# Four modulation rows of a second layer computed in the grid attention instead of the latent attention

## The reference, cut to what matters

```python
for i in range(DEPTH):
    m_lat = jnp.split((c_lat @ w_mod[i] + b_mod[i])[:, None, :], N_MOD, axis=-1)   # N_MOD = 6, w_mod: 2 x 1024 x 6144
    m_ctx = jnp.split(c_con @ w_mod[i] + b_mod[i], N_MOD, axis=-1)
    h_lat = modulate(x_lat, g_pre_mix[i], m_lat[0], m_lat[1])
    ...
    x_lat = x_lat + m_lat[2] * rms_norm(y_lat, g_post_mix[i])
    f_lat = channel_mlp(modulate(x_lat, g_pre_mlp[i], m_lat[3], m_lat[4]), w_mlp_in[i], w_mlp_out[i])
```

## Time and profile before

| what | value |
|---|---|
| three runs, median (lowest to highest) | 2287.1 us (2286.93 to 2288.31) |
| profiled execution: its own time, its span | 2291.53 us, 2290.2 us |
| busy PE | 2230.3 us, 97% of the span |
| busy DVE, ACT, POOL | 1240.3 us (54%), 1019.6 us (45%), 565.2 us (25%) |
| chain that ended last, by engine | PE 77%, DVE 10%, POOL 6%, ACT 5% |
| mean granted TensorE clock | 0.994 of full speed |
| moved by DMA | 344.54 MB, 149 GB/s over the span |

### The profile page before, as it was taken

The page is one execution under the profiler, slowest core; times in us unless marked ns, Lnnn a source line. Parts: engine busy times, 40 slices in busy tenths (PEclk is TensorE's granted clock), DMA queues, the critical chain, the costliest instruction groups (busy, mean ns, idle before and its releaser), DMA issues.

```text
span 2290.2 us, 34957 instructions
## 1 busy us (share of the span) xinstructions
PE 2230.3 (97%) x15237; PEld 1958.2 (86%) x15237; DVE 1240.3 (54%) x1486; ACT 1019.6 (45%) x1226; POOL 565.2 (25%) x465
## 2 busy tenths in 40 slices
PE   9999899999999999999999999999999999999999
PEld 8889898978889889778889966898888898678999
DVE  5766566657655665477556456352223264565443
ACT  5544345445543454455444366343322334554442
POOL 3323444331330231231232210011211200231221
PEclk9999999999999999999999999999999999999999
DMA  8555445456555555786555310132232242114552
GB/s 282 184 175 184 158 147 165 155 199 200 188 187 188 177 197 167 255 300 219 181 189 178 102 38 19 40 127 92 92 106 96 92 142 74 56 60 162 184 184 74
DMA packets 205234, 344.54 MB, mean 150 GB/s; under 512 B 8845, under 2 KB 69498, under 8 KB 205082
## 3 DMA queue, kind: packets, MB, share of 16 engines
q1 hardware_dynamic: 205082, 342.31, 45.6%
HBM read 341.24 MB, written 1.05 MB: 149 GB/s over the span
## 4 chain that ended last, share of the span: by engine, by line
PE 77%; DVE 10%; POOL 6%; ACT 5%; issue 2%; SPq 0%; DMA 0%; DVEq 0%; POOLq 0%; ACTq 0%
PE PS L472 74%; DVE WL L458 4%; PE PS L494 3%; ACT WH L442 2%; POOL small L1682 1%; POOL small L1680 1%; POOL TMP L1691 1%; POOL TMP L1076 1%; DVE TMP L1594 1%; DVE small L1572 0%; POOL TMP L1692 0%; DVE TMP L1047 0%; DVE TMP L1044 0%; DVE XB L704 0%; DVE TMP L1039 0%
## 5 line engine op out<-in xcount | busy, mean ns | idle before, releaser
L458 DVE TENSOR_TENSOR WL<-raw,WH 128x2048 fp32r<-128x2048 f32 (+2 forms) x281 | 653.7, 2347 | 651.6 <-ACT WH L442 651.6
L472 PE MATMUL PS<-XB,WH 128*128 128x256 f32 (+1 forms) x3392 | 898.6, 342 | 3.8 <-DVE XB L1138 1.1
L472 PE MATMUL PS<-XB,WL 128*128 128x256 f32 (+1 forms) x2368 | 687.9, 290 | 0.0
L472 PEld LDWEIGHTS PS<-XB,WH 128*128 128x128 f32 x3392 | 585.5, 189 | 84.1 <-issue 4.1
L442 ACT ACTIVATE WH<-raw 128x2048 fp32r<-128x2048 f32 (+2 forms) x281 | 515.5, 1858 | 263.7 <-PE PS L472 258.2
L472 PEld LDWEIGHTS PS<-XB,WL 128*128 128x128 f32 x2368 | 448.3, 189 | 8.7
L472 PE MATMUL PS<-WH,XB 128*128 128x256 f32 (+2 forms) x1888 | 379.2, 296 | 13.6 <-DVE WL L458 10.2
L472 PE MATMUL PS<-HB,WH 128*128 128x256 f32 (+1 forms) x1568 | 344.1, 309 | 1.0 <-DVE WL L458 1.0
L472 PEld LDWEIGHTS PS<-WH,XB 128*128 128x128 f32 x1888 | 306.3, 193 | 35.7 <-issue 16.0
L472 PE MATMUL PS<-WL,XB 128*128 128x256 f32 (+2 forms) x944 | 275.7, 292 | 0.0
L472 PEld LDWEIGHTS PS<-HB,WH 128*128 128x128 f32 x1568 | 255.7, 191 | 18.9 <-DVE WL L458 3.0
(11 more groups left out here) (256 smaller groups left out, 2189.3 us busy)
## 6 DMA issues: line engine op xcount, KB each, us to landing
raw<-in_ffn_w_in SPq DMA_DIRECT2D x88, 1024.0 KB, 5.2
raw<-in_w_mod SPq DMA_DIRECT2D x48, 1024.0 KB, 5.3
raw<-in_ffn_w_out SPq DMA_DIRECT2D x40, 1024.0 KB, 5.2
raw<-in_a_w_in SPq DMA_DIRECT2D x36, 1024.0 KB, 5.1
raw<-in_w_mlp_in SPq DMA_DIRECT2D x32, 1024.0 KB, 5.2
raw<-in_w_mlp_out SPq DMA_DIRECT2D x32, 1024.0 KB, 5.1
raw<-in_gla_w_in SPq DMA_DIRECT2D x12, 1024.0 KB, 5.2
raw<-in_attn_w_qkv SPq DMA_DIRECT2D x6, 1024.0 KB, 5.1
```

Source lines behind the costliest of these rows:

```text
L458: dve.e.tensor_tensor(self.WL[j % NRAW][:, 0:nk * nn], self.raw[j % NRAW][:, 0:nk * nn], wh.bitcast(F32), ALU.subtract).then_inc(*self.lo. ...
L472: return self.pe.e.matmul(out, l, r, start=start, stop=stop, skip_group_check=skip)
```

## The change

Latent attention: in steps -1, 0, 1 and 2 one modulation row less is placed on PE, ACT and DVE. Step -1 keeps two, steps 0 to 2 keep the first of two, step 3 keeps both. Grid attention: one row each is placed in the steps 25, 27, 29 and 31, on PE at the end of the step, on ACT behind the step's exponentials, on DVE in the step after, behind its scores. All four use bank 0 for the matmuls and bank 1 for the transposes. ACT copies the last one in step 33. The order of the rows stays, so the rows that move are the sixth to ninth of the second layer by number, which the gated linear attention and the second MLP use. The chunks of the moved rows stand in the stream between the last projection of the grid attention and its output projection now.

```diff
--- before.py
+++ after.py
@@ -1819,15 +1819,14 @@
             if own:
                 turn_p(hs, 2)
                 turn_p(hs, 3)
-            fill()
+            if hs not in (0, 1, 2):
+                fill()
             if own:
                 pv(hs, 2)
                 pv(hs, 3)
             if more:
                 turn(hs + 1, 1)
-            if hs < 0:
-                fill()
-            else:
+            if own:
                 self.empties([7], (self.o_done, ("lat", hs)))
         self.attn_out_pe("lat", self.aO, (self.o_done, ("lat", 3)), w_out)
 
@@ -1942,15 +1941,13 @@
                 self.fill_act(0)
                 self.act_settle()
                 turn(hs + 1, 0)
-            self.act_held = int(not more)
-            self.fill_act(0)
-            self.act_held = 0
-            self.act_settle()
+            if hs not in (0, 1, 2):
+                self.act_held = int(not more)
+                self.fill_act(0)
+                self.act_held = 0
+                self.act_settle()
             if more:
                 turn(hs + 1, 1)
-            if hs < 0:
-                self.fill_act(0)
-                self.act_settle()
         self.attn_out_act("lat", "f3", 40)
 
     def latent_dve(self):
@@ -2084,11 +2081,11 @@
                 turn_p(hs, 3)
             if more:
                 rotated(1, hs + 1)
-            self.dve_held = int(not more)
-            fill()
-            self.dve_held = 0
+            if hs not in (0, 1, 2):
+                self.dve_held = int(not more)
+                fill()
+                self.dve_held = 0
             if hs < 0:
-                fill()
                 continue
             dve.wait_ge(self.expd, ("lat", hs, 3))
             dve.e.reciprocal(rd, den).then_inc(*self.v_step.up(("lat", "recip", hs)))
@@ -2600,6 +2597,7 @@
 
 
 
+    GRID_FILLS = (25, 27, 29, 31)
     GRID_SPARE = {6: 2, 2: 3, 3: 6}
 
     GRID_STEPS = [(seg, 2 * pair + j, o) for seg in range(2) for pair in range(2) for o in range(2) for j in range(2)]
@@ -2756,6 +2754,8 @@
                 g, p = divmod(n - 2, 8)
                 for j in range(2):
                     turn_p(g, 2 * p + j)
+            if n in self.GRID_FILLS:
+                self.pe_mods.send((0, 1))
         self.rest_grid = self.last_products_pe("grid", w_o, self.x_both(("go0", "go1")), None, True)
 
     def grid_act(self):
@@ -2862,8 +2862,12 @@
             if n < 32:
                 score(g, 2 * p)
                 score(g, 2 * p + 1)
+            if n in self.GRID_FILLS:
+                self.fill_act(0)
             if p == 0:
                 next(nxt, None)
+            if n == 33:
+                self.act_settle()
             if 27 <= n < 33:
                 seg, g3 = divmod(n - 27, 3)
                 split(g3, seg)
@@ -2936,6 +2940,8 @@
             g, p = divmod(n, 8)
             if n < 32:
                 score(g, 2 * p)
+            if n - 1 in self.GRID_FILLS:
+                self.dve_mods.send(1)
             if n > 5 and n % 4 == 2:
                 out(*divmod(n // 4 - 1, 2))
             if n and n % 4 == 0:
```

## The result

The changed kernel takes 2319.28 us (2312.26 to 2323.21), the kernel before 2287.05 on the same chip: 1.0132 [1.0117, 1.0146], or 32 us by the medians. The profiled execution of after took 2312.26 us (span 2310.9), 20.7 more than the profiled execution of before.

A forecast was written before the change was run, and what follows sets the result against it. PE was taken to bound the kernel, so a move pays only where PE waits. Latent -1.5 plus grid +18.7 gave +17.2 us on the median of 2287.1: 2304.3 us, range 2296 to 2312.

The forecast's parts named there:

- The order on the lists: Latent and grid attention: places of splits and copies in the engines' lists cost -1.5 + 18.7 = +17.2 us together.
- Head 0: Latent attention, step -1: ACT splits in time, PE begins head 0 at about 970.3, gain 3.0 us.
- the scaling: Latent step 0: DVE's scaling, behind two splits, begins at 990.4 against 986.82; PE idles 3.4 us; step 1.7 us later.
- -1.5: Latent attention sum in us: -3.0 + 1.7 + 1.7 - 1.9, within a bound of -10.3 and +2.
- the first two terms: Grid attention: row at 25 costs +2.3 us, row at 27, waiting for ACT's copy, +4.6.
- 18.7: Grid attention sum in us: rows 2.3 + 4.6 + 5.4 + 4.4, and late output projection splits 2.0.
- The loads: Grid attention: loads of the moved rows' and the projection's chunks cost nothing, by the count of buffers.
- rival (3): Both attentions: clock falls behind PE's new waits; one or two falls of 5.1 us, 2309 to 2314 us; chance 0.20.
- (1): Grid attention: ACT's copies reach PE in time, rows cost only their work, +12.2 us, some 2297.8; chance 0.17.
- (2): Both attentions: cover holds, grid idle takes 4.43 us, latent gives back 10.3; -4.4, 2282.7 us; chance 0.10.

The follow-up runs named there:

- fillers: Changed kernel plus dummy matmuls on PE in the waits the change made, in both latent and grid attention: 2306.36 us, 1.0076 to the kernel before.
- the second trace: Trace of the changed kernel run once more, unaltered, beside the kernel before on another group's chip: 2316.63 us, 1.0125.
- late splits and early copies: Changed kernel with latent weight splits held past the first row, grid row copies ahead of the exponentials, output projection's splits apart: 2292.11 us, 1.0022.

## Why the prediction was wrong, by its own steps

**The order on the lists: right, term by term.** Head 0 was to begin 3.0 us earlier in step -1; it begins at 971.61 in after, 3.1 earlier once the 1.37 us by which the whole latent attention starts later are taken off. In step 0 the scaling was to begin at 990.4 and PE to wait for 3.4 us; 988.63 in after is 990.4 once moved by the 1.75 us that lie between the two starts of head 0, and the wait is 3.37. With fillers "latent" is 1.9 us shorter, against -1.5. In the grid, on the trace with fillers: scores behind the row at 27 6.8 us later than before (sum of the first two terms: 6.9), scores behind the row at 29 12.2 (12.3), products of step 30 behind the row at 31 and the splits 18.4 (18.7). The loads were free, as counted: no wait of PE, ACT or DVE in the grid of after is put down to a load.

**The step that failed: the clock of the sum.** Every term was taken at a granted clock of 1.00, and the fall of the clock was kept apart as rival (3) with a chance of 0.20 and a size of one or two falls of 5.1 us. It was the case that came, and larger than it was sized: 2319.28 us lies above its 2314 too. The first trace of after has four falls in the two places; they lengthen "latent" by 6.4 us and "grid" by 1.6, the second trace 5.4 and 5.1. By the ratios the executions pay 11 to 13 us for the missing fillers, so some us probably lie in falls that these two traces don't have: the traced execution of the first comparison had a mean granted clock of 0.991, the three others 0.985 to 0.988. Where these lost their time is not shown. Both traces of after, and every other one here that leaves the latent waits unfilled, show the clock fall behind both of them (waits of 3.16 to 3.37 us, 8 of 8).

**Why it was weighed wrongly.** Against rival (3) stood the clock of 1.00 through the idle of the last group. But those pieces are 0.24 to 0.88 us long, and the waits that the change adds are 1.9 to 3.4: the row to weigh was the one of a wait of that size, 2.16 us in the earlier trace rows, with a fall behind it. The Trainium skill ("TensorE: Matmul & The Clock Gate", section "HAM oscillation — how this bites in real kernels") tells of a matmul kernel in which every wait for data is long enough to drop the clock, so that each burst starts slow. The runs agree for the waits above 3 us (8 of 8). Below that it is not each time: in the four traces with the grid's waits unchanged, a fall begins behind the wait of 1.90 us in 4, behind 2.93 in 1, behind 2.33 in 3.

**The rivals (1) and (2).** The copies are a wait, as the traces of PE show. The cover does not hold by itself; late splits and early copies make it hold in the latent attention (8.6 of 10.3 us), not in the grid.

**What stays open.** Which waits between 1.76 and 2.93 us cost the clock: the length alone doesn't say, since 1.90 does more often than 2.93. And the 11 to 13 us between the changed kernel and the one with fillers are followed only in the traced executions. These are 7.5 and 12.0 us longer than the traced one with fillers, and the two places together are 8.0 and 10.5 us longer in them; the slower executions of the changed kernel have no trace.

## What to carry to other kernels

Before you move work off a full engine, list what counts position by chunks or steps (here the splits two chunks ahead) and where it lands in every other engine's list. Putting the splits back alone made the latent attention 13.0 us shorter with the clock and 6.7 without, where the moved work is 10.3. Where a change makes the matmul engine wait some 2 us or more, put the clock into the forecast and not into a rival: look for a wait of that size in the trace and read the granted clock behind it. The place that paid here for loose work is where the kernel runs dummy matmuls, and only once the copy that frees the bank stood early in its engine's list.

## What the runs showed of the hardware

One program with one order of work differs by 11 us between executions (2312.26 to 2323.21; mean granted clock 0.991 to 0.985). That is no property of the changed kernel alone: the kernel before lay within 1.4 us in the four runs beside it, but 15 executions of it on another chip lie between 2285.82 and 2295.67 us (0.996 to 0.992). A place in the grid attention that no edit touches shows one way. In all 14 traces PE waits 1.76 us there; behind it the clock falls in 5 of them and stays at 1.00 in 9. Timelines of PE, kernel before and kernel with fillers in the latent attention:

```profile
1326.09 1.72 PE L472 MATMUL PS<-al,al 64*128 64x512 f32 x12 [1.76 <-DVE small L2899]
```

```profile
1325.44 2.85 PE L472 MATMUL PS<-al,al 64*128 64x512 f32 x12 [1.76 <-DVE small L2905]
```

And work that computes nothing made the changed kernel 11 to 13 us faster by the ratios: dummy matmuls in waits of 1.9 to 3.4 us.
